# Both MLP layers by nested seven-product levels in one run of 56 quarter products, outer weight sums on GpSimd

## The reference, cut to what matters

```python
D_MODEL = 1024
D_FF = 4 * D_MODEL
...
    x = x + merged @ p['w_out']
    hm = _rmsnorm(x, p['norm_mlp'])
    x = x + jnp.square(jax.nn.relu(hm @ p['w_mlp_in'])) @ p['w_mlp_out']
```

## Time and profile before

| | us |
|---|---|
| median of 3 runs | 2486.44 |
| lowest, highest | 2486.03, 2491.84 |
| profiled execution | 2496.8 |
| its span, first to last instruction | 2495.0 |
| TensorE busy | 2334.2 (94%) |
| VectorE busy | 1449.7 (58%) |
| ACT busy | 787.0 (32%) |
| GpSimd busy | 263.0 (11%) |

### The profile page before, as it was taken

One profiled execution on the slowest core, in us unless ns is written; L12 is line 12 of the kernel. 1 busy time (PEld: TensorE's weight loads), 2 busy tenths in 40 slices (PEclk: granted clock), 3 DMA queues, 4 the chain that ended last, 5 costly groups with the idle time before them and its releaser, 6 DMA issues. The chain is left out here.

```text
span 2495.0 us, 48708 instructions
## 1 busy us (share of the span) xinstructions
PE 2334.2 (94%) x19499; PEld 1746.0 (70%) x19499; DVE 1449.7 (58%) x2969; ACT 787.0 (32%) x1393; POOL 263.0 (11%) x242
## 2 busy tenths in 40 slices
PE   6999999999899989897999889999999999999997
PEld 4566788765656566665666668787888888888886
DVE  3256888974556564336566656648934744644643
ACT  4134888424334341324454532121200200200101
POOL 0020000000000000001001101124202203302300
PEclk8998999999999999899899999999999999999999
DMA  6441232343132313237877745416503703702512
GB/s 186 120 118 51 73 105 70 121 150 101 46 112 58 96 46 97 83 106 217 270 232 257 243 166 170 146 41 202 176 18 111 227 17 95 235 26 63 151 34 81
DMA packets 295486, 306.76 MB, mean 123 GB/s; under 512 B 56487, under 2 KB 216072, under 8 KB 295133
## 3 DMA queue, kind: packets, MB, share of 16 engines
q1 hardware_dynamic: 220148, 252.78, 32.3%
q10 hardware_dynamic: 75112, 50.87, 7.2%
HBM read 239.78 MB, written 62.23 MB: 121 GB/s over the span
## 5 line engine op out<-in xcount | busy, mean ns | idle before, releaser
L1286 PE MATMUL rwkv_banks<-gate_sides_then_att_T 128*128 128x384 f32 (+1 forms) x768 | 281.9, 500 | 7.8 <-PEq L441 3.7
L2969 DVE TENSOR_TENSOR x<-x,ps_mm 128x272 f32<-128x272 f32 x280 | 120.2, 436 | 283.6 <-PE ps_mm L2934 283.5
L2934 PE MATMUL ps_mm<-merged_then_hidden,w_mm 128*128 128x272 f32 x960 | 227.7, 393 | 1.3 <-DVE sums_of_right_sides_ L3482 1.1
L2934 PEld LDWEIGHTS ps_mm<-merged_then_hidden,w_mm 128*128 128x128 f32 x960 | 182.2, 190 | 39.6 <-DVE sums_of_right_sides_ L3482 1.5
L1286 PEld LDWEIGHTS rwkv_banks<-gate_sides_then_att_T 128*128 128x128 f32 x768 | 139.4, 197 | 75.9 <-issue 18.1
L3598 DVE TENSOR_TENSOR merged_then_hidden<-merged_then_hidden,ps_mm 128x544 f32<-128x544 f32 x180 | 128.0, 716 | 108.1 <-PE ps_mm L3338 107.8
L2934 PE MATMUL ps_mm<-sums_of_right_sides_,w_sums_mm 128*128 128x272 f32 x704 | 165.3, 392 | 1.0 <-DVE sums_of_right_sides_ L3438 1.0
L2934 PEld LDWEIGHTS ps_mm<-sums_of_right_sides_,w_sums_mm 128*128 128x128 f32 x704 | 133.7, 190 | 28.9 <-issue 1.4
L600 PE MATMUL first_banks<-hT,w_pr 128*128 128x384 f32 (+3 forms) x432 | 149.0, 504 | 3.8 <-PEq L188 3.8
L910 DVE TENSOR_SCALAR_CACHE_REDUCE _and_tildes_then_k_pages<-scores,mid 128x384 f32<-128x384 f32 (+4 forms) x150 | 131.5, 877 | 3.1
L600 PEld LDWEIGHTS first_banks<-hT,w_pr 128*128 128x128 f32 (+1 forms) x432 | 83.1, 197 | 63.8 <-issue 24.3
(11 more groups left out here) (592 smaller groups left out, 4570.1 us busy)
## 6 DMA issues: line engine op xcount, KB each, us to landing
v_pages<-in_cache_v SPq DMA_DIRECT2D x128, 256.0 KB, 5.3
gate_sides_then_att_T<-in_w_in ACTq DMA_DIRECT2D x46, 512.0 KB, 4.2
gate_sides_then_att_T<-right_blocks_d SPq DMA_DIRECT2D x83, 272.0 KB, 2.8
_and_tildes_then_k_pages<-in_cache_k SPq DMA_DIRECT2D x88, 256.0 KB, 3.3
right_blocks<-right_blocks_d SPq DMA_DIRECT2D x64, 272.0 KB, 2.8
T_and_gates_then_weights<-in_w_mlp_in SPq DMA_DIRECT2D x16, 1024.0 KB, 5.9
w_mm<-in_w_mlp_out SPq DMA_DIRECT2D x32, 512.0 KB, 4.9
w_pr<-in_w_in SPq DMA_DIRECT2D x27, 512.0 KB, 5.2
```

Source lines behind the costliest of these rows:

```text
L1286: ins = MM(B[:, gate_bank(n), 0:w], gw[:, n % 2, k_, :], hc[:, k_, 0:w], start=(k_ == 0), stop=(k_ == KO - 1))
L2934: ins = self.nc.tensor.matmul(self.ps[:, 2 * self.BANK[step] + c, 0:272], left[step][:, k, :], right[step][:, k, 272 * c:272 * c + 272], s ...
L2969: self.nc.vector.tensor_tensor(to, to, ps, ALU.add).then_inc(self.by_dve, 1)
```

## The change

- Layer two becomes nested too: 7 quarter products of 7 products instead of 4 units of 14 products. The `Halves` units of the MLP and `second_weights`, `second` are gone.
- The eight layers (two in each round) form one run of 56 quarter products, 392 products, with one interlocking order from the first to the last. `UP` is the order of the quarter products in a first layer, `DOWN` in a second one, `TAIL` in the last.
- Each layer loads four weight quarters into the same `quarter` buffers, when the layer before has used them. Those of second layers aren't scaled.
- The four outer weight sums of every layer, 32 operations of 128x2048, are made by GpSimd (`weight_sums` stands in its block), woven between the inner sums.
- In a second layer the right blocks come from the hidden activations. VectorE makes them (`right_blocks`, 28 a layer). t1 to t4 are written over the hidden activations once the blocks that need them have been read.
- Results of a second layer are gathered in 128x544 pieces into `result`: P2, P3 and P4 straight into `x1`, and P1, P5, P6, P7 into their own accumulators (y1, y5, y6, y7) over all four rounds. `spread_results` adds these together and to `x1` in the last layer: 16 operations of 1088 elements.
- In first layers ACT copies P1's result on (`copy_first`), and in the first second layer it writes the first results of P1, P7, P5 and P6.

The core of the diff:

```diff
+    UP, DOWN, TAIL = (("P1", "P2", "P6", "P7", "P4", "P5", "P3"), ("P1", "P2", "P3", "P7", "P5", "P4", "P6"),
+                      ("P1", "P2", "P3", "P5", "P6", "P7", "P4"))
+    layers = [UP, DOWN] * (R - 1) + [UP, TAIL]
+    names = [name for order in layers for name in order]
...
+    def at(q, step):
+        return STEP * f.place[q, step]
...
+            def weight_sums():
...
+                for n in range(2 * R):
+                    yield at(7 * n - 2, "P4") + STEP + 2.0 if n else -14.0
+                    if n:
+                        pool.wait_ge(*f.product(nth[n - 1]["P5"], "P4"))
...
+                    has(n, "a21")
+                    has(n, "a22")
+                    G.tensor_tensor(s1, a21, a22, ALU.add).then_inc(l_summed, 1)
+                    yield at(7 * n - 2, "P4") + STEP + 2.1 if n else 5.0
...
+                    G.tensor_tensor(a21, a11, a21, ALU.subtract).then_inc(l_summed, 1)
+                    yield at(7 * n - 1, "P4") + STEP + 0.9 if n else 9.0
...
+                    G.tensor_tensor(s2, s1, a11, ALU.subtract).then_inc(l_summed, 1)
+                    yield at(7 * n - 1, "P4") + STEP + 4.0 if n else 26.0
...
+                    G.tensor_tensor(s4, a12, s2, ALU.subtract).then_inc(l_summed, 1)
+
+            def all_inner_sums():
+                for q in range(1, 14 * R):
+                    yield at(q - 1, "P5") + 2.0 if q > 1 else 0.0
+                    inner_sums(q)
+
+            weave(weight_sums(), all_inner_sums())
...
-            for r in range(R):
-                for q, step in f.SEQ[:-1]:
-                    product(r, q, step)
...
-                d.multiply(pe, ML + r * H2, h_right, hidden_ready, opened, lambda: product(r, *f.SEQ[-1]))
-                for j in range(1, H2):
-                    d.multiply(pe, ML + r * H2 + j, h_right)
+            for q, step in f.seq:
+                product(q, step)
...
-            def weight_sums():
-                a11, a12, a21, a22 = (quarter[n] for n in ("a11", "a12", "a21", "a22"))
...
+            def spread_results():
+                last = nth[2 * R - 1]
+                for after, step, pairs in (("P1", "P4", ((x11, y1),)), ("P5", "P4", ((x12, y5), (x22, y5))),
+                                           ("P6", "P4", ((y6, y1), (x12, y6))),
+                                           ("P7", "P4", ((y7, y6),)), ("P4", "P3", ((x21, y7), (x22, y7)))):
...
-            weave(merge_out(), x_sums(), x_blocks(), weight_sums(), rstds(), gather(), finish(), hidden_sums(),
-                  second())
-            dve.wait_ge(*d.nth_kept(N - 1, "P4", 1))
+            weave(merge_out(), x_sums(), right_blocks(), rstds(), gather(), finish(), hidden_sums(),
+                  spread_results())
```

524 lines of the change are left out of this document (251 added, 273 removed).

## The result

| | kernel before | changed kernel |
|---|---|---|
| median, us (lowest to highest) | 2487.26 (2486.03 to 2491.84), 4 runs | 2536.49 (2529.71 to 2541.22), 4 runs |
| ratio, 95% interval | 1 | 1.018 (1.0157 to 1.0203) |
| profiled execution, us | 2496.8, span 2495.0 | 2541.2, span 2539.4 |
| matmuls of TensorE | 19499 | 19275 |

What follows compares the result with a forecast made beforehand. TensorE was taken to bound the MLP: -54.4 fewer products, +7.5 first layers, +76 and +4 second layers, +4 round 0, +7 the end, sum +44 us, median 2530 (range 2472 to 2575; likeliest case 2500 to 2555).

Steps and rivals of the forecast that it cites:

- Fewer products: Whole MLP: 98 products a round instead of 105, 51.3 us less; with the unit starts' 3.1 less, -54.4 together.
- GpSimd's 4.5 us for 2048 elements: On GpSimd: each 128x2048 outer weight sum takes 4.5 us, carried from two smaller sizes; bounds 3.8 and 5.1.
- the layout: Hand-laid order of VectorE and GpSimd turns: TensorE loses 18 us per second-layer start, rounds 1 to 3, before the clock.
- Second layers: Starts of second layers: turns delay gathers, 16 us in round 0, 20 each later, +76; t2, t4 sums +4.
- First layers: Starts of first layers, rounds 1 to 3: GpSimd's queue makes inner sums late, 2.4 us each, +7.5 (0 to 15).
- Round 0, first layer: Round 0's first layer: x sums wait behind outer sums, 11 us with the clock against 7.3 before, +4 (0 to 10).
- The end: Last layer's end: adding y7 to x21 and x22 +3, three quarter products before it +4, together +7 (3 to 12).
- What would show it: Trace signs of being right: GpSimd rows 4.4 us or more, VectorE blocks 3 to 5, gather-ended gaps 3 to 7.
- The first (VectorE let in during a long operation): Second layers: GpSimd gives way inside a long sum, so they cost 14 in all; total -24, 2462 us; chance 0.17.
- The second (slack absorbs more): Second layers: slack absorbs more than laid out, 8 to 10 us each, 2480 to 2500 in total; chance 0.09.
- the third: First and second layers: 5.1 us per sum, ties against VectorE, low clock; +36 more, 2566, up to 2590; chance 0.14.
- The fourth: Steady state: the 51.3 us saving doesn't come, TensorE meets other waits; 24 quarters at 1 us; chance within 0.14.

Runs made afterwards that it cites:

- third experiment: Changed kernel with the outer weight sums left out but for 8 elements each: 2455.3 us, ratio 0.9861 to the kernel before.
- fourth experiment: Kernel before with its own 16 outer weight sums moved from VectorE to GpSimd, between the inner sums: 2490.4 us, ratio 0.9995.
- second experiment: Changed kernel with each outer weight sum replaced by constant fills on GpSimd of about the same time, reading nothing: 2497.8 us, ratio 1.0012.
- seventh experiment: Changed kernel with outer weight sums one by one, each ahead of the quarter product that wants it, instead of in pairs: 2508.9 us, ratio 1.0055.
- tenth experiment: Changed kernel without the additions that carry the last layer's shared results into the others (spread_results): 2529.4 us, ratio 1.0158.

## Why the prediction was right, point by point

The sum was made by rounds, so it can be compared by rounds. Before, by the starts of TensorE's rows, the rounds took 203.5, 193.4, 193.5 and 193.6 us; after, by the stage table, 209.4, 201.8, 200.9 and 214.8.

| round | forecast | measured |
|---|---|---|
| 0 | -12.8 - 0.8 + 4 + 16 + 1 = +7.4 | +5.9 |
| 1 | -12.8 - 0.8 + 2.5 + 20 + 1 = +9.9 | +8.4 |
| 2 | +9.9 | +7.4 |
| 3 | +9.9 + 7 = +16.9 | +21.2 |
| all | +44.1 | +42.9 |

The rest of the 44.4 lies in the final norm, whose first transposes ran at a granted clock of 0.66, 5.51 us instead of the 3.68 of the earlier trace rows:

```profile
2516.86 5.51 PE L3682 MATMUL y_ps<-ident,x 128*128 128x128 f32 x32 [1.13 <-PEq L3129]
```

*Fewer products.* Right: without outer sums a first layer takes 89.8 us and a second one 92.0 for 49 products (third experiment), and the unit starts are gone.

*GpSimd's 4.5 us for 2048 elements.* Right: 4.51 to 4.53 us in the quiet, in the changed kernel's shortest and in the fourth experiment's. With turns it is 4.8 to 5.6, which I had inside the layout. Here is the row of all eight s1 (shortest, median and longest in ns):

```profile
L3262 POOL TENSOR_TENSOR w_mm<-T_and_gates_then_weights x8: 4518/4998/5590, 1693.3 to 2396.5; 128x2048 f32<-128x2048 f32 x8
```

*Second layers.* The mechanism was right and the price nearly so. I had 17 us in round 0 and 21 in the others with t2 and t4; the excess over 89.8 is 15.2, 17.4 and 16.9, and some 19 in the last, 30.4 less 11. That is 69 against 80: 11 too much, a seventh. The layout had a gap at every one of the first gathers. On the chip the first ones were absorbed, and the loss came in three gaps (one of 8.9 and two small ones in round 0), the longest behind t1 and t3, which I had as the last and least: I had laid them beside an inner set, and they ran beside s2 and s4. The 2 us for the clock were too few: products behind these gaps took 2.93, 3.79 and 3.76 us instead of 2.0 as recorded, and the second one behind the first gap 2.89, some 5.4 us in this layer. So more slack and a dearer clock cancel in part, which is luck. How the price divides was also not as I had it: of 15 to 17 us a layer some 9 to 11 go with the reading and some 4 to 5.5 with the queue alone (the second experiment against the third; I had 3.5).

*First layers.* Mechanism right, size too small: 4.4 to 4.8 us instead of 2.5, 14 against 7.5 in three. TensorE waits where I had said, on the inner sums behind each pair of outer sums (2.2 and 2.1 us, L3235), and further small waits and a slow product come on top. The seventh experiment shows that this part is the pairing's: with sums one by one a first layer loses 0.9 us, 0.65 of it in one gap. The second shows that it is the queue's and not the turns': with fills it stays (4.2 to 5.8 us).

*Round 0, first layer.* 104.4 - 89.8 = 14.6, with 2 us of the small matmuls that add the squares: 12.5 against the 11 of my layout. Part of the way was another: a 2.6 us gap at 1700.71 is ended by ACT. Its copy of a result from PSUM stood in its queue behind the new `copy_first`, which waited for a gather that an x sum of 5.04 us beside s1 had held up. I had ACT down as having room to spare; it has, but its order passes a delay on.

*The end.* The term that was mis-sized most: 11 us by the tenth experiment against 7. I had priced three quarter products at 4 us in all; each of two costs 1.85 + 1.62, and the last one 0.55 + 2.13 and a slow product.

*What would show it.* Sums of over 4.4 us, blocks at 3.6 and 3.8, and gaps in four clusters, ended by gathers: as written, but for the gaps' sizes, 2.6 to 4.7 us and 8.9 once instead of 3 to 7. The last product ends at 2515.7, not at 2508. By the rule of the Trainium skill, "SBUF — State Buffer", section "Who interferes with whom", the trace agrees: 0.71 becomes 3.77 beside a sum that reads, and stays 0.72 beside fills that only write.

*The rivals.* The first (VectorE let in during a long operation) falls with the 3.77 and 7.23 us rows. Its time was too low besides: the second experiment, in which VectorE never waits for an outer sum, stands at 1.0012 of the kernel before, and the rival had 2462, 0.990, since first layers, the end and round 0 cost more than it had for them. The second (slack absorbs more) was true in a small way, the third too (first layers and the end dearer, the clock), and they cancelled, which is why the sum is better than its terms. The fourth is excluded by the third experiment. What stays open is why the medians lie 49 us apart and the profiled executions 44: with four runs each and a spread of 11.5 us in the changed kernel's, that can't be told from chance.

## What to carry to other kernels

Before a sum moves from VectorE to GpSimd, add up for the stretch in which it must be done all time of both engines' operations that have their inputs in SBUF: the two exclude each other, so it is one resource, and where its total came near the stretch's length, as in the second layers here, cutting and reordering mostly chose who was late. Then price GpSimd's queue by itself: it cost nearly as much here (1.5 points) as the reading (1.7). An operation is late also for what it has queued in front of: look for gathers behind it. And an order without a wait does not place anything in time; an engine with nothing ahead runs on and meets the very work that it was moved away from.
